# A fused two-block kernel: other places for the first gate logits, the gates and two pair products of the gated linear attention

## The reference

```python
def gla_chunked(q, k, v, logg):
    ...
    b = jnp.cumsum(logg, axis=3)
    qe = q * jnp.exp(b)
    ke = k * jnp.exp(-b)
    a = jnp.einsum('bhncd,bhnjd->bhncj', qe, ke)
    a = jnp.where(mask, a, 0.0)
    o_intra = jnp.einsum('bhncj,bhnjv->bhncv', a, v)
    ...

def gla_mixer(h, w_in, w_gate_up, b_gate, out_g, w_o):
    proj = h @ w_in
    q, k, v, r, z = jnp.split(proj, ...)
    logit = jnp.einsum('bsir,ire->bsie', z, w_gate_up.astype(f32)) + b_gate.astype(f32)
    logg = (jax.nn.log_sigmoid(logit) / GATE_TAU).reshape(B, S, 2, GLA_HEADS, GLA_DK)
    o_f = gla_chunked(q, k, v, logg[:, :, 0])
    o_b = flip(gla_chunked(flip(q), flip(k), flip(v), flip(logg[:, :, 1])))
    o = rmsnorm(o_f + o_b, out_g).reshape(B, S, GLA_V)
    o = o * jax.nn.silu(r.astype(f32))
    return o.astype(h.dtype) @ w_o
```

## Time and profile before

| | us |
|---|---|
| median of 3 runs (918.3 to 919.76) | 918.45 |
| the profiled execution, whole | 918.71 |
| its span, first to last instruction | 916.8 |
| TensorE busy | 895.8 |
| VectorE busy | 622.5 |
| ScalarE busy | 493.0 |
| mean granted TensorE clock | 0.995 |

### The profile page before, as it was taken

One profiled execution on the slowest core, in us unless ns is written; L12 is line 12 of the kernel. 1 busy time (PEld: TensorE's weight loads), 2 busy tenths in 40 slices (PEclk: granted clock), 3 DMA queues, 4 the chain that ended last, 5 costly groups with the idle time before them and its releaser, 6 DMA issues.

```text
span 916.8 us, 17451 instructions
## 1 busy us (share of the span) xinstructions
PE 895.8 (98%) x7219; PEld 838.3 (91%) x7219; DVE 622.5 (68%) x993; ACT 493.0 (54%) x731; POOL 0.2 (0%) x4
## 2 busy tenths in 40 slices
PE   5999999999999999999999999999999999999997
PEld 4888787999999999889999999999999999999896
DVE  4786666777767776997755555566977755555554
ACT  3449655755555567875643333366657654433333
POOL 0000000000000000000000000000000000000000
PEclk8999999999999999999999999999999999999999
DMA  9997869564564588334655555456353555555541
GB/s 325 363 323 255 279 217 365 198 236 171 182 227 167 170 193 169 89 93 139 208 186 184 184 185 184 146 184 194 127 167 126 168 184 184 184 184 184 184 138 46
DMA packets 133883, 176.34 MB, mean 192 GB/s; under 512 B 20864, under 2 KB 113452, under 8 KB 133804
## 3 DMA queue, kind: packets, MB, share of 16 engines
q1 hardware_dynamic: 132844, 173.05, 58.1%
q10 hardware_dynamic: 960, 2.16, 0.7%
HBM read 174.16 MB, written 1.05 MB: 191 GB/s over the span
## 4 chain that ended last, share of the span: by engine, by line
PE 80%; DVE 6%; ACT 5%; DMA 4%; SPq 2%; issue 2%; ACTq 0%; DVEq 0%
PE psum L1739 24%; PE psum L1731 20%; PE psum L1732 20%; PE psum L1735 4%; PE psum L1736 4%; DMA raw<-in_w_in_dram 2%; DVE w_lo L1049 2%; ACT w_hi L592 2%; DMA arena<-in_w_ada_dram 2%; PE psum L1841 1%; PE psum L2270 1%; PE psum L2291 1%; DMA raw<-in_w_ada_dram 1%; PE psum L2280 1%; PE psum L2341 1%
## 5 line engine op out<-in xcount | busy, mean ns | idle before, releaser
L1731 PE MATMUL psum<-h_hi,w_hi 128*128 128x256 f32 x1352 | 329.0, 283 | 3.7 <-DVE w_hi L1242 2.4
L592 ACT ACTIVATE w_hi<-raw 128x2048 fp32r<-128x2048 f32 x135 | 256.9, 1905 | 135.3 <-PE psum L1739 115.6
L1732 PE MATMUL psum<-h_lo,w_hi 128*128 128x256 f32 x1352 | 325.3, 280 | 0.0
L1049 DVE TENSOR_TENSOR w_lo<-raw,w_hi 128x2048 fp32r<-128x2048 f32 x135 | 304.0, 2277 | 22.2 <-ACT w_hi L592 22.0
L1731 PEld LDWEIGHTS psum<-h_hi,w_hi 128*128 128x128 f32 x1352 | 255.2, 189 | 10.0 <-issue 4.8
L1732 PEld LDWEIGHTS psum<-h_lo,w_hi 128*128 128x128 f32 x1352 | 256.1, 189 | 0.8
L1739 PE MATMUL psum<-h_hi,w_lo 128*128 128x256 f32 x1352 | 186.1, 280 | 1.0 <-DVE w_lo L1049 0.9
L1739 PEld LDWEIGHTS psum<-h_hi,w_lo 128*128 128x128 f32 x1352 | 169.7, 188 | 1.8 <-DVE w_lo L1049 1.6
L1453 DVE SCALAR_TENSOR_TENSOR arena<-psum,rstd 128x256 f32<-128x256 f32 x64 | 26.9, 423 | 132.3 <-PE psum L1739 130.4
L1731 PE MATMUL psum<-a_hi,w_hi 128*128 128x256 f32 x464 | 110.7, 281 | 0.7 <-DVE a_lo L1440 0.5
L1732 PE MATMUL psum<-a_lo,w_hi 128*128 128x256 f32 x464 | 110.3, 279 | 0.0
(11 more groups left out here) (286 smaller groups left out, 909.9 us busy)
## 6 DMA issues: line engine op xcount, KB each, us to landing
raw<-in_mlp_w_in_dram SPq DMA_DIRECT2D x32, 1024.0 KB, 5.6
raw<-in_mlp_w_out_dram SPq DMA_DIRECT2D x32, 1024.0 KB, 7.2
raw<-in_w_up_dram SPq DMA_DIRECT2D x22, 1024.0 KB, 5.2
raw<-in_w_ada_dram SPq DMA_DIRECT2D x20, 1024.0 KB, 7.7
raw<-in_gla_w_in_dram SPq DMA_DIRECT2D x12, 1024.0 KB, 5.3
raw<-in_w_down_dram SPq DMA_DIRECT2D x11, 1024.0 KB, 5.5
raw<-in_w_in_dram SPq DMA_DIRECT2D x6, 1024.0 KB, 9.1
arena<-in_w_ada_dram SPq DMA_DIRECT2D x4, 1024.0 KB, 12.7
```

What stands on the lines that cost most here:

```text
L592: act.activation(chunk(w_hi, m % SPLIT_SLOTS, SPLITS[m]), chunk_raw(r % RAW_SLOTS, SPLITS[m]), ACT.Copy).then_inc(*mark("w_hi", m))
L1049: dve.tensor_tensor(chunk(w_lo, m % SPLIT_SLOTS, key), chunk_raw(r % RAW_SLOTS, key), chunk(w_hi, m % SPLIT_SLOTS, key).bitcast(F32), ALU. ...
L1731: pe.matmul(dst, high, both[0], start=start, stop=False, skip_group_check=True)
L1732: return pe.matmul(dst, high, both[1], start=False, stop=False, skip_group_check=True)
```

## The change

Only the list of steps changes, for the GLA layer. Nothing is added or removed; the same instructions stand in another order.

```diff
-            s += [("gla_in", 0), ("gla_in", 1), ("gla", 2), ("gla_in", 2), ("logits", 0), ("gla", 3), ("gate", 0),
-                  ("gla_in", 3), ("gla", 4), ("gate", 1), ("gla_in", 4), ("logits", 1), ("gla", 5),
-                  ("keys", 0), ("r_cols", 5), ("gate", 2), ("gla_in", 5)]
-            s += [("gla", 6), ("keys", 1), ("gate", 3), ("gla_in", 6), ("gla", 7), ("keys", 2), ("mix", 0),
-                  ("gla_in", 7), ("keys", 3), ("gla", 8), ("mix", 1), ("gla_in", 8), ("gla", 9), ("gla_in", 9), ("mixed", 0),
+            s += [("gla_in", 0), ("gla_in", 1), ("gla", 2, 0), ("logits", 0), ("r_cols", 5), ("gate", 0), ("gla", 2, 1),
+                  ("gla_in", 2), ("gla", 3), ("gate", 1), ("gla_in", 3), ("gla", 4), ("logits", 1), ("gla_in", 4), ("gate", 2),
+                  ("gla", 5), ("keys", 0), ("gla_in", 5), ("gate", 3)]
+            s += [("gla", 6), ("keys", 1), ("gla_in", 6), ("gla", 7), ("keys", 2),
+                  ("gla_in", 7), ("gla", 8), ("mix", 0), ("mix", 1), ("gla_in", 8), ("keys", 3), ("gla", 9), ("gla_in", 9), ("mixed", 0),
```

## The result

| | kernel before | changed kernel |
|---|---|---|
| median (us) | 918.76 (918.30 to 920.11, 11 runs) | 922.16 (919.40 to 925.44, 11 runs) |
| profiled execution (us) | 918.7 | 919.4 |
| its span (us) | 916.8 | 917.6 |

The changed kernel is slower, by a ratio of 1.0033 with a 95% interval of 1.0024 to 1.0043. That is 3.4 us at the median, where 1.2 us was forecast, and the median lies outside the predicted range. The profiled execution of the changed kernel is not typical: at 919.4 us it is the lowest of its 11 runs, and the other ten lie from 921.14 to 925.44. So its profile can show what happens to the order of the work, and it can miss what makes the other runs slow.

What follows compares the result with a forecast made beforehand. TensorE, busy for 895.8 of 916.8 us, was taken as the bound. +2.49 us at chunk 7, -0.35 at chunk 8 and -0.92 at chunk 9 made +1.2 us, giving 919.7 us, range 917.3 to 921.2.

Steps and rivals of the forecast that it cites:

- The waits, and where they go: TensorE's waits for `w_lo`: chunk 7 gets one of 2.87 us; 0.35 in chunk 8 and 0.92 in chunk 9 go.
- The gates' distance: Gate starts on ScalarE stay 7.97 us apart, with 0.71 us more before gate 3 for two copies of v.
- the 5.0 us to VectorE's next instruction: VectorE is free for the `w_lo` behind a gate 5.0 us after that gate starts on ScalarE.
- The starts of the gates: Gates 0 to 3 start on ScalarE at 627.56, 635.5, 643.5 and 652.2 us.
- The sum of delays: Whole kernel: +2.49 us at chunk 7, -0.35 at chunk 8, -0.92 at chunk 9, together +1.2 us.
- The column beside the logits: Norm column run with logits 0 on TensorE: saves 0.35 us (bounds nothing and 0.4), which drops out behind a later wait.
- the clock falls in the new wait: Rival: TensorE's clock drops in chunk 7's new idle time, costing at most 3.4 us, so 923.1; chance 9%.
- The new wait isn't there: Rival: chunk 7's `w_lo` is ready in time, old waits and column's ends are won, -1.6 us, so 916.8; chance 10%.
- The gates take longer: Rival: each gate takes 0.4 us more on ScalarE and VectorE, chunk 7's `w_lo` comes 1.6 us later, 921.3; chance 11%.

Runs made afterwards that it cites:

- filled: The changed kernel plus 22 matmuls of unused result filling TensorE's wait ahead of chunk 7's low-weight matmuls: 919.81 us, ratio 1.0019.
- fill_10: The changed kernel plus 10 matmuls of unused result in chunk 7's wait, leaving 1.57 us idle: 919.86 us, ratio 1.0010.
- no_wait: The changed kernel with gate 3 moved behind the `w_lo` of chunk 7 and keys 1 behind that of chunk 8: 916.72 us, ratio 0.9980.
- the two repetitions: The changed kernel measured twice more with no edit: 921.27 us (ratio 1.0034) and 922.52 us (ratio 1.0034).
- fill_4: The changed kernel plus 4 matmuls of unused result in chunk 7's wait, leaving 2.29 us idle: 922.71 us, ratio 1.0039.
- The repetition: The changed kernel measured once more with no edit, the first such time: 921.27 us, ratio 1.0034; its profiled execution took 921.96 us.
- long_wait: The changed kernel with keys 1 also ahead of the `w_lo` of chunk 7 on VectorE: 924.36 us, ratio 1.0064.

## Why the prediction was wrong

**The waits, and where they go: right.** L1739 waits once, in chunk 7, and not in chunks 8 and 9. The gates' distance, the 5.0 us to VectorE's next instruction and the `w_lo` held. The forecast was a wait of 2.87 us beyond the steady distance. The trace has 659.17 - 656.14 - 0.12 = 2.91. The starts of the gates are all 0.3 to 0.4 us earlier than forecast, but the landmark came 0.57 us earlier in that execution. Behind the landmark gate 0 starts at 2.20 us (627.19 - 624.99), where the forecast has 2.00 (627.56 - 625.56), so the chain is 0.2 us late from its first gate on. The 2.91 is near the 2.87 because TensorE came later as well: at chunk 7 it had saved 0.18 us and not 0.35.

**The sum of delays: right in the main.** +1.2 was forecast; filled, which has the delay and no idleness, took +1.45 by medians and +1.40 from the landmark, fill_10 +1.23 by medians and +1.38 from the landmark. The positions behind the landmark show where the missing 0.2 us went. Chunk 7 goes on at 34.18 us for 31.45 in the kernel before, +2.73 where 2.49 was forecast: that is gate 0. Against it stands a price that the prediction left out. Behind a wait the tile's next high-weight matmul follows 1.05 us after the first low-weight one (659.17 to 660.22) and not 0.94, so each wait costs another 0.11 us. The kernel before has two of these, for chunk 8:

```profile
664.38 1.22 PE L1739 MATMUL psum<-w_lo,h_hi 128*128 128x256 f32 x8 [0.19 <-DVE w_lo L1049]
665.43 0.28 PE L1735 MATMUL psum<-w_hi,h_hi 128*128 128x256 f32 x1
```

and likewise for chunk 9. The changed kernel has one: 2.73 + 0.11 - 1.27 - 0.22 = 1.35, for 1.37 measured.

**The column beside the logits: its size held, half of it was lost again.** The kernel before has these tiles around logits 0 and around the column:

```profile
628.38 1.10 PE L1739 MATMUL psum<-h_hi,w_lo 128*128 128x256 f32 x8
...
632.45 1.09 PE L1739 MATMUL psum<-h_hi,w_lo 128*128 128x256 f32 x8
...
647.77 1.10 PE L1739 MATMUL psum<-w_lo,h_hi 128*128 128x256 f32 x8
...
651.33 1.11 PE L1739 MATMUL psum<-w_lo,h_hi 128*128 128x256 f32 x8
```

Against steady tiles (2.80 and 2.84 us) the logits cost 1.27 us and the column 0.72. Merged they cost 629.40 - 624.99 - 2.82 = 1.59, so 0.40 us is saved. But 0.22 of it goes at chunk 6, whose `w_lo` the prediction called tight (done at 650.8, wanted at 651.0). It comes about 0.1 us late, and the wait costs its 0.11 besides:

```profile
650.24 0.28 PE L1736 MATMUL psum<-w_hi,h_lo 128*128 128x256 f32 x1
650.47 1.22 PE L1739 MATMUL psum<-w_lo,h_hi 128*128 128x256 f32 x8
651.52 0.28 PE L1735 MATMUL psum<-w_hi,h_hi 128*128 128x256 f32 x1
```

no_wait has the same loss there. Its gain of 1.67 us is 1.27 + 0.22 + 0.40 - 0.22, so two terms that the prediction left out cancel.

**The rival "the clock falls in the new wait": this is the step that failed.** It was given 9%, and the range ended below it. Its mechanism is what happened in three profiled executions of four that had an idle time of 2.29 to 2.75 us (the two repetitions and fill_4), and by times in most runs: of the 23 runs of the changed kernel one lies under 921, and their mean granted clocks speak for about one fall a run. What failed was the argument against it: "the new idle time stands alone in dense work, while the one at the start lay in thin work". The row gave a drop behind 2.43 us of idleness, the new idle time was longer, and nothing in the trace showed that dense work on both sides protects. It doesn't. The rows of before held no idle time of that length in dense work, so the one row near it deserved a much larger share of the chance than a tenth, and the range had to reach 923.

**Its price: right in kind, and mostly too high.** At most 3.4 us was said, from 6.8 us at the lower level. After a wait of 2.75 us the clock was low for 3.4 us and not 6.8, partly while nothing was ready to run, and the cost was 1.3 to 1.5 us in the profiles. The row at the start that gave the 6.8 wasn't typical either. The wait there is 2.4 us in all twelve profiled executions; in the kernel before and in the first of the changed kernel the clock is low for 6.8 us behind it, in the other ten for 3.4. The repetition has, against the earlier trace rows:

```profile
15.00:20.00 5.00, 2.57 (x15) 2.49 (x15) 3.85 (x8) 2.16 (x4) 0.00 (x0) 0.82 1.10 348
20.00:25.00 5.00, 5.00 (x52) 3.41 (x51) 1.50 (x6) 1.79 (x4) 0.00 (x0) 0.83 1.07 369
```

At the median over filled it was 1.46 on the chip where both ran. The changed kernel's first 11 runs lie 3.4 us above their kernel before, 1.95 more than filled does above its own on another chip. The fall in the profiles accounts for 1.4 of it, the longer low times in some runs or the scatter ahead of the landmark possibly for the rest.

The Trainium skill, page "TensorE: Matmul & The Clock Gate", section "Why this matters for your kernels", warns that an idle gap between bursts of matmuls sends the clock back to half, but it means gaps somewhat longer than this one. The runs here agree that a gap does so and differ on its length: behind 2.75 us it fell in two profiles of three, behind 2.29 us in the one. So by the page this rival wasn't the likely one; what spoke for it was the row at the start, with a fall behind 2.43 us.

**The other two rivals.** "The new wait isn't there" didn't come true, but its price did: no_wait took 916.72 for the 916.8 of that rival. "The gates take longer" was false, since they stand 8.0 us apart. Its price (921.3) also lay just outside the range, which the prediction doesn't say.

What stays open: why the first profiled execution kept its clock behind the same idle time; where the runs of 922.5 to 925.4 us have their further 3.4 us or so at the lower level (6.8 us in one piece, as behind long_wait's 5.25 us of idleness, would fit their times, but no profile of the changed kernel shows it); and why the transfers of the first 200 us keep TensorE waiting longer in some executions.

## What to carry to other kernels

Cost a new wait of TensorE twice: the delay, by the chain that feeds it, and then the clock, which in three profiles of four behind idle times of 2.29 and 2.75 us was low for 3.4 us in the midst of dense work. A step that is moved ahead on VectorE must be followed to the first product behind it that TensorE needs, and that product goes first: moving a gate and a keys step back behind the weights turned a loss of 3.4 us into a gain of 1.6. When executions of a kernel scatter by more than the effect, compare the profiles from a landmark ahead of the edit, and don't take a single profile for the typical run.

## What the runs showed of the hardware

- The clock fell behind a single idle time of 2.75 us (two profiles of three) and of 2.29 us (one of one) in the middle of dense matmuls. It didn't in the profiles with 1.57, 1.54 and 1.37 us. Of the 33 runs of those kernels four lie 1.1 us or more above their medians (1.4 to 1.8); of the 27 runs of the kernel before beside them five do, so that is the scatter of every kernel. At 1.92 us one profile of one has no fall, and the times speak for some.
- It stayed at the 1.2 GHz level for 3.4 us in all three of those profiles, and for 6.8 us behind 5.25 us of idleness. What that costs depends on how much of it lies in the idle time itself: 1.3 and 1.4 us where the fall came before the end of the wait, 1.5 where it came after.
- The same wait of 2.4 us at the start of the program left the clock low for 3.4 us in ten profiled executions and for 6.8 in two, so the low time behind one wait isn't a constant.
- Behind a wait of any length here (0.19 to 2.75 us, clock at 1.00) the first eight matmuls held the next one up by 0.11 us more than in steady work: 1.05 us for 0.94.
- Useless matmuls in a wait kept the clock at 1.00, and ten of them (1.3 us) did as well as 22.
